# Turned value products on probabilities scaled in place by ScalarE, and the last normalization ahead of the third selection

## Chip, cores and metric

One core of a Trainium2 chip runs the whole kernel, one decoder block for 512 positions. The metric is the device time of one execution in microseconds.

## What is computed

After an input normalization, one projection of the 512 x 1024 stream feeds a diagonal state-space branch and a sparse attention branch; sigmoid gates join them, a second projection and a normalization follow, then a router sends each position to 4 of 32 experts. The parts that the change touches are the attention's softmax and value product, and the router's selection:

```python
logits = einsum('bqhd,bqkhd->bhqk', qb, k_sel) * HEAD_DIM ** -0.5
logits = logits - slopes[None, :, None, None] * dist[:, None]
logits = where((dist >= 0)[:, None], logits, -inf)
p = softmax(logits, axis=-1)
out = einsum('bhqk,bqkhd->bqhd', p, v_sel)          # 8 heads of 64
...
mix = (g_ssm * y_ssm + g_att * y_att) @ w_o
h = layer_norm(alpha * h + mix, ln1_g, ln1_b)
logits = h @ w_router + b_router
top_val, top_idx = top_k(logits, 4)
gates = softmax(top_val, axis=-1)
```

## The kernel before, in words

The program is written out engine by engine; each engine works through its own list in order, and semaphores (`s_...`) order the engines among each other. Positions are tiled by 128 into four query tiles t = 0..3.

Attention (349.6 to 458.1 us) runs over 32 steps i = (t, head). A step's keys are the t + 1 chunks of 128 positions up to its own tile, so its width is 128, 256, 384 or 512 columns. On TensorE: `qk` (L1548) makes the query-key products of two steps at once, each on 64 rows of the array; `probsT` (L1560) transposes the probabilities of a step, chunk by chunk, into bank 7; `pv` (L1570) multiplies the transposed probabilities (stationary, 128 columns) with the values (moving, 64 columns), so the result has queries on partitions; after a query tile's eight heads `o_T` (L1580) transposes its output in four pieces. Between the steps, at every even i, TensorE puts one tile of the gated linear unit (GLU) of the state-space branch: 12 products of 512 columns (L1431 to L1433). On VectorE: `logits` (L1093) adds the distance penalty, takes the row maximum and scales it; after a query tile it takes the reciprocals of the eight sums and multiplies the output with them (L1123, L1126). `value` (L1106) multiplies a GLU tile with its gate. On ScalarE: `exps` (L782) is the exponential with its row sum, `keep_pT` (L790) copies bank 7 to the memory of the transposed probabilities, `take` (L721) is the sigmoid of a GLU gate tile, which needs another activation table than the exponential. The probabilities and their transposes have two buffers each.

The order in the loops is what matters. TensorE at step i: `qk(i)` if i is even, a GLU tile if i is even, `probsT(i - 1)`, `pv(i - 2)`. ScalarE at step i: `exps(i)`, `keep_pT(i - 1)`, and `take` where i % 4 is 3. VectorE at step i: `logits(i)`, and `value` where i % 4 is 1.

The GLU's weights are split by GpSimd into an upper and a lower part (L550, L552), one split for each GLU tile.

After the attention come its output projection (L1437) and the joined output projection `w_out` (L1610), to 541.5 us. VectorE then normalizes tile t (L1171 to L1181), TensorE transposes it and multiplies with the router's weights (`route`, L1626), VectorE selects the four experts (L1188 to L1202), TensorE counts the places (`place`, L1643), and VectorE marks which positions go in the first expert's rows (L1150) and computes the addresses of all (`first_addresses`, L1146, eight small instructions a tile). GpSimd writes a list of positions for each expert by these addresses (`write_first`, L582, four scattered writes a tile, each tile as its addresses come). SyncE loads the finished list, VectorE takes the next block's positions from it (`next_token`, L1280), and only then goes on with the split (`lo`, L1160) of part 7 of the first expert's weights. The first block uses weight parts 4 to 11 (1 MB each): ScalarE rounds the upper part (`hi`, L827), VectorE subtracts it (`lo`), and TensorE multiplies (`up_part`, L1719). `first_rows` (L1659) gathers the first expert's rows by a product with the marks. Then 32 blocks and a last one follow, each with 12 weight parts.

## Time and profile before

| | |
|---|---|
| three runs, median (lowest to highest) | 1761.35 us (1761.05 to 1763.37) |
| the profiled execution, its own time | 1764.82 us |
| its span | 1763.1 us |
| TensorE busy | 1686.9 us, 96% of the span |
| VectorE, ScalarE, GpSimd busy | 1499.1, 1063.4, 467.5 us |
| chain that ended last, by engine | TensorE 87%, VectorE 9%, ScalarE 2% |

The chain is followed back from the last instruction, at each step to what released it. An engine that is not on it may still be idle or busy without changing the end. The granted clock of TensorE is printed as a share of full speed: 1.00 is 2.4 GHz, 0.50 is 1.2 GHz. Instructions overlap a little in the records, so what one costs in a queue is the distance between two starts rather than its own length.

### The profile page before, as it was taken

The page shows a single profiled execution, that of the slowest core. Times are in us where ns is not written, and L with a number is a line of the kernel's source. Part 1 is how long each engine was busy: PE and PEld are TensorE (multiplying, and loading weights), DVE is VectorE, ACT ScalarE, POOL GpSimd, SP SyncE. Part 2 cuts the span into 40 slices and gives each one's busy share as a digit, 9 for nine tenths or more (in the row PEclk, how much of TensorE's full clock was granted, in tenths as well). Part 3 has the DMA queues.
Part 4 walks back from the last instruction along what each step waited for, and adds up shares of the span by engine and source line. Part 5 has one row for each costly group of instructions (what it writes and reads, how often), then busy time and mean ns, then how long its engine had stood idle before and what let it go on. Part 6 is the DMA issues. An engine that isn't in the chain of part 4 may idle for free.

```text
span 1763.1 us, 22201 instructions
## 1 busy us (share of the span) xinstructions
PE 1686.9 (96%) x7129; PEld 1107.8 (63%) x7129; DVE 1499.1 (85%) x1710; ACT 1063.4 (60%) x1016; POOL 467.5 (27%) x298
## 2 busy tenths in 40 slices
PE   5899999999997999999999999999999999999996
PEld 2333344476576577777777777777777777777763
DVE  5999877555568799999999999999999999999995
ACT  4332222365445477777777777777777777777771
POOL 4855000064334111223121212222222212121210
PEclk9999899998998899999999999999999999999998
DMA  5111122110316789999999999999999999999973
GB/s 172 48 51 48 48 76 92 58 48 39 120 45 227 304 308 369 368 366 366 368 382 358 368 365 378 361 365 360 373 365 369 364 371 374 363 355 373 382 293 104
DMA packets 91901, 464.76 MB, mean 264 GB/s; under 512 B 21289, under 2 KB 21405, under 8 KB 42616
## 3 DMA queue, kind: packets, MB, share of 16 engines
q1 hardware_dynamic: 80240, 441.67, 65.9%
q0 software_dynamic: 9776, 18.41, 4.3%
q10 hardware_dynamic: 1848, 4.24, 0.7%
q8 instruction: 17, 0.28, 0.1%
q14 instruction: 20, 0.16, 0.0%
HBM read 454.15 MB, written 18.53 MB: 268 GB/s over the span
## 4 chain that ended last, share of the span: by engine, by line
PE 87%; DVE 9%; ACT 2%; issue 1%; DMA 0%; ACTq 0%; DVEq 0%
PE ps L1715 20%; PE ps L1717 20%; PE ps L1716 20%; PE ps L1515 6%; PE ps L1701 3%; PE ps L1442 2%; PE ps L1437 2%; PE ps L1723 2%; PE ps L1423 2%; PE ps L1431 1%; PE ps L1623 1%; PE ps L1622 1%; PE ps L1621 1%; PE ps L1576 1%; PE ps L1433 1%
## 5 line engine op out<-in xcount | busy, mean ns | idle before, releaser
L1163 DVE TENSOR_TENSOR w_lo<-raw,w_hi 128x2048 fp32r<-128x2048 f32 x384 | 874.1, 2287 | 76.3 <-ACT w_hi L832 76.2
L832 ACT ACTIVATE w_hi<-raw 128x2048 fp32r<-128x2048 f32 x384 | 737.0, 1920 | 244.6 <-PE ps L1717 244.2
L1715 PE MATMUL ps<-w_hi,x_hi 128*96 128x512 f32 x1024 | 415.9, 406 | 0.0
L1717 PE MATMUL ps<-w_lo,x_hi 128*96 128x512 f32 x1024 | 404.7, 395 | 0.0
L1716 PE MATMUL ps<-w_hi,x_lo 128*96 128x512 f32 x1024 | 404.4, 395 | 0.0
L1715 PEld LDWEIGHTS ps<-w_hi,x_hi 128*96 128x96 f32 x1024 | 169.3, 165 | 67.5 <-issue 1.5
L1717 PEld LDWEIGHTS ps<-w_lo,x_hi 128*96 128x96 f32 x1024 | 166.7, 163 | 71.1 <-issue 0.2
L1715 PE MATMUL ps<-w_hi,a_hi 128*96 128x512 f32 x512 | 204.6, 400 | 5.7 <-DVE a_lo L1261 5.7
L1716 PEld LDWEIGHTS ps<-w_hi,x_lo 128*96 128x96 f32 x1024 | 167.0, 163 | 64.0 <-issue 0.2
L1716 PE MATMUL ps<-w_hi,a_lo 128*96 128x512 f32 x512 | 201.8, 394 | 0.0
L604 POOL DMA_INDIRECT gate_now<-gate_rows,row_now x32 | 79.8, 2495 | 458.8 <-DVE tok_out L1291 443.7
L1717 PE MATMUL ps<-w_lo,a_hi 128*96 128x512 f32 x512 | 201.5, 394 | 0.0
L612 POOL DMA_INDIRECT sum_rows<-far,tok_out x31 | 77.2, 2489 | 335.7 <-ACT far L918 335.7
L1442 PE MATMUL ps<-ring 128*128 128x512 f32 x256 | 120.1, 629 | 2.5 <-ACT ring L686 2.0
L1515 PE MATMUL ps<-ring 128*128 128x512 f32 x256 | 111.5, 595 | 0.0
L1715 PEld LDWEIGHTS ps<-w_hi,a_hi 128*96 128x96 f32 x512 | 83.0, 162 | 39.2 <-issue 5.8
L1717 PEld LDWEIGHTS ps<-w_lo,a_hi 128*96 128x96 f32 x512 | 83.1, 162 | 36.3
L1716 PEld LDWEIGHTS ps<-w_hi,a_lo 128*96 128x96 f32 x512 | 83.3, 163 | 33.4
L1442 PEld LDWEIGHTS ps<-ring 128*128 128x128 f32 x256 | 50.8, 202 | 71.6 <-issue 69.3
L596 POOL DMA_INDIRECT scr<-h_rows,tok_now x32 | 70.5, 2205 | 81.3 <-DVE tok_now L1285 74.3
L1515 PEld LDWEIGHTS ps<-ring 128*128 128x128 f32 x256 | 48.2, 190 | 61.5 <-issue 61.2
L918 ACT ACTIVATE far<-ps,gate_now 96x512 f32<-96x512 f32 x64 | 40.3, 678 | 42.7 <-PE ps L1717 42.7
(323 smaller groups left out, 2034.6 us busy)
## 6 DMA issues: line engine op xcount, KB each, us to landing
raw<-in_w_up SPq DMA_DIRECT2D x256, 1024.0 KB, 8.0
raw<-in_w_down SPq DMA_DIRECT2D x128, 1024.0 KB, 9.4
ring<-in_w_in SPq DMA_DIRECT2D x9, 2048.0 KB, 7.8
ring<-in_w_glu SPq DMA_DIRECT2D x4, 1024.0 KB, 6.3
ring<-in_w_o SPq DMA_DIRECT2D x2, 2048.0 KB, 11.7
h<-in_x SPq DMA_DIRECT2D x4, 512.0 KB, 4.9
ring<-in_w_attn_proj SPq DMA_DIRECT2D x1, 2048.0 KB, 8.9
h_rows<-h ACTq DMA_DIRECT2D x4, 512.0 KB, 3.6
```

Source lines behind the costliest of these rows:

```text
L596: g.indirect_dma_start(xg[:, :], None, h1_rows, bass.IndirectOffsetOnAxis(ap=tok_now[:, 0:1], axis=0), bounds_check=last_tok, oob_is_err=F ...
L604: g.indirect_dma_start(gate_now[:, :], None, gate_rows, bass.IndirectOffsetOnAxis(ap=row_now[:, 0:1], axis=0), bounds_check=last_row, oob_ ...
L612: g.indirect_dma_start(sum_rows, bass.IndirectOffsetOnAxis(ap=tok_out[:, 0:1], axis=0), ysb.rearrange("p a b -> p (a b)"), None, bounds_ch ...
L832: s.activation(hi_of(c)[:, :], raw_of(c), ACT.Copy).then_inc(s_hi, 1)
L918: s.activation(ysb[:, r, :], ps[4 + r][0:BLK, :], ACT.Copy, scale=gate_now[:, 0:1]).then_inc(s_ysb, 1)
L1163: d.tensor_tensor(lo_of(c)[:, :], raw_of(c), hi_of(c)[:, :], ALU.subtract).then_inc(s_lo, 1)
L1442: ins = mm(o[:, :], w[:, k, c:c + P], hT[:, k, :], start=k == 0, stop=k == KD - 1)
L1515: ins = mm(ps[n % 2][:, :], gate_weights(g)[:, k, :], hT[:, k, :], start=k == 0, stop=k == KD - 1)
L1701: ins = tr(ps[bank][:, BLK * k:BLK * k + BLK], cols(k), ident[0:BLK, 0:BLK])
L1715: mm(o, xh, hi_of(c)[:, col], start=start, stop=False)
L1716: mm(o, xl, hi_of(c)[:, col], start=False, stop=False)
L1717: return mm(o, xh, lo_of(c)[:, col], start=False, stop=stop)
```

## The change

In the attention the probabilities and their transposes get four buffers each. ScalarE scales each step's probabilities in place by the reciprocal of their sum (`norm`), which VectorE now takes step by step (`inverse`), so that VectorE's normalization of the output and TensorE's transposes of it go. The value products are turned: the values (64 columns) are stationary, the transposed probabilities (128 columns) move, and two heads write to the two halves of the output partitions (`pv_pair`), so that the output comes out transposed. ScalarE copies it once per query tile (`keep_oT`). The orders of the three loops shift: TensorE has the GLU tile at odd i, `probsT(i - 2)` and `pv_pair(i - 4)`; ScalarE has `norm(i - 1)`, `keep_pT(i - 2)` and `take` where i % 4 is 2; VectorE has `inverse(i - 1)` and `value` where i % 4 is 0.

In the routing VectorE normalizes tile 3 right after tile 2, ahead of the selection for tile 2; the marks are parted from the addresses, and the addresses of tiles 1 to 3 are computed together after the last marks, in five wider instructions. ScalarE's and TensorE's lists follow. The dense gates are transposed into bank 4 instead of bank 1, and TensorE waits for them after two weight parts instead of ahead of the first; its wait for the addresses goes.

```diff
@@ -162,8 +162,8 @@
         w_st = [scr[:, 8:12], scr[:, 12:16], ring[:, 5, 1536:3584].rearrange("p (k t) -> p k t", k=4),
                 far[:, :, :], gb[:, :, :].rearrange("p r (k t) -> p (r k) t", k=2)]
         score, relu = scr[:, 0:2], scr[:, 2:4]
-        logit, prob, pT, glu_t = scr[:, 4:6], scr[:, 6:8], scr[:, 8:10], scr[:, 10:12]
-        oq, mix_t = scr[:, 12:13], scr[:, 13:16]
+        logit, glu_t, prob, pT = scr[:, 4:6], scr[:, 6:8], scr[:, 8:12], scr[:, 12:16]
+        mix_t = scr[:, 4:5]
         top8 = sb("top8", [P, 8])
         amax = sb("amax", [P, 2])
         rsum = sb("rsum", [P, TT, HEADS])
...
@@ -782,34 +782,45 @@
             def exps(i):
                 t, hh = STEPS[i]
                 act.wait_ge(s_lg, i + 1)
-                if i >= 2:
-                    act.wait_ge(s_pTp, i - 1)
-                s.activation(prob[:, i % 2, 0:NQT[t]], logit[:, i % 2, 0:NQT[t]], ACT.Exp, scale=HD ** -0.5,
+                if i >= 4:
+                    act.wait_ge(s_pTp, i - 3)
+                s.activation(prob[:, i % 4, 0:NQT[t]], logit[:, i % 2, 0:NQT[t]], ACT.Exp, scale=HD ** -0.5,
                              bias=amax[:, i % 2:i % 2 + 1], accum_out=rsum[:, t, hh:hh + 1]).then_inc(s_pr, 1)
 
             def keep_pT(i):
                 t, hh = STEPS[i]
                 act.wait_ge(s_pTp, i + 1)
-                if i >= 2:
-                    act.wait_ge(s_pv, i - 1)
-                s.activation(pT[:, i % 2, 0:NQT[t]], ps[7][:, 0:NQT[t]], ACT.Copy).then_inc(s_pT, 1)
+                if i >= 4:
+                    act.wait_ge(s_pv, (i - 4) // 2 + 1)
+                s.activation(pT[:, i % 4, 0:NQT[t]], ps[7][:, 0:NQT[t]], ACT.Copy).then_inc(s_pT, 1)
+
+            def norm(i):
+                t, hh = STEPS[i]
+                act.wait_ge(s_inv, i + 1)
+                s.activation(prob[:, i % 4, 0:NQT[t]], prob[:, i % 4, 0:NQT[t]], ACT.Copy,
+                             scale=rinv[:, hh:hh + 1]).then_inc(s_pn, 1)
+
+            def keep_oT(t):
+                act.wait_ge(s_pv, HEADS // 2 * (t + 1))
+                s.activation(qiT[:, :, P * t:P * t + P], ps[2 + t % 2][:, :].rearrange("p (k q) -> p k q", k=4),
+                             ACT.Copy).then_inc(s_oT, 1)
 
             for i in range(len(STEPS) + 2):
                 if i < len(STEPS):
                     exps(i)
                 if 1 <= i <= len(STEPS):
-                    keep_pT(i - 1)
-                if i % 4 == 3 and n < first_tile["at"]:
+                    norm(i - 1)
+                if i >= 2:
+                    keep_pT(i - 2)
+                if i % 4 == 2 and n < first_tile["at"]:
                     take(n)
                     n += 2
-                if i >= 2 and STEPS[i - 2][1] == HEADS - 1:
-                    t = STEPS[i - 2][0]
-                    act.wait_ge(s_oTp, t + 1)
-                    s.activation(qiT[:, :, P * t:P * t + P], ps[3][:, :].rearrange("p (k q) -> p k q", k=4),
-                                 ACT.Copy).then_inc(s_oT, 1)
+                if i >= 11 and STEPS[i - 11] == STEPS[HEADS * ((i - 11) // HEADS)]:
+                    keep_oT((i - 11) // HEADS)
             while n < first_tile["at"]:
                 take(n)
                 n += 2
+            keep_oT(TT - 1)
...
-            for t in range(TT):
+            def std(t):
                 act.wait_ge(s_var, TT + t + 1)
                 s.activation(rsx[:, t, 0:1], mvx[:, t, 1:2], ACT.Sqrt, bias=eps[:, 0:1]).then_inc(s_rstd, 1)
-                if t == 1:
-                    act.wait_ge(s_bs, 1)
-                    step(s.activation(bias3[third, :], braw_b[third, :], ACT.Copy))
-                    s.activation(brem[third, :], bias3[third, :], ACT.Copy).then_inc(s_bc, 1)
-                if t == 2:
-                    step(s.activation(bias3[second, :], braw_b[second, :], ACT.Copy))
-                    act.wait_ge(s_bs, 2)
-                    s.activation(bias3[third, :], braw_b[third, :], ACT.Copy).then_inc(s_b3l, 1)
-                if t == 3:
-                    for c in range(4, 6):
-                        hi(-1, c)
+
+            def rows_off(t):
                 act.wait_ge(s_h1, t + 1)
                 act.dma_start(h1_rows.rearrange("(t p) d -> p t d", p=P)[:, t, :], h[:, t, :]).then_inc(s_h1row, 16)
+
+            def keep_hT1(t):
                 for r in range(2):
                     act.wait_ge(s_h1T, 2 * t + r + 1)
                     if t > 0:
                         act.wait_ge(s_lgt, t)
                     s.activation(hT1[:, 4 * r:4 * r + 4, :], ps[6 + r][:, :].rearrange("p (k q) -> p k q", k=4),
                                  ACT.Copy).then_inc(s_h1e, 1)
+
+            def gate_exps(t):
                 act.wait_ge(s_v8, t + 1)
                 s.activation(all_exp[:, t, :], lg[:, :], ACT.Exp, bias=gneg[:, 0:1])
                 s.activation(gates[:, t, :], rt8[:, t, 0:TOPK], ACT.Exp, bias=gneg[:, 0:1],
                              accum_out=gsum[:, 0:1]).then_inc(s_ge, 1)
+
+            std(0)
+            rows_off(0)
+            keep_hT1(0)
+            gate_exps(0)
+            std(1)
+            act.wait_ge(s_bs, 1)
+            step(s.activation(bias3[third, :], braw_b[third, :], ACT.Copy))
+            s.activation(brem[third, :], bias3[third, :], ACT.Copy).then_inc(s_bc, 1)
+            rows_off(1)
+            keep_hT1(1)
+            gate_exps(1)
+            std(2)
+            step(s.activation(bias3[second, :], braw_b[second, :], ACT.Copy))
+            act.wait_ge(s_bs, 2)
+            s.activation(bias3[third, :], braw_b[third, :], ACT.Copy).then_inc(s_b3l, 1)
+            rows_off(2)
+            keep_hT1(2)
+            std(3)
+            gate_exps(2)
+            rows_off(3)
+            keep_hT1(3)
+            hi(-1, 4)
+            gate_exps(3)
+            hi(-1, 5)
+
...
@@ -1103,6 +1135,11 @@
                 d.tensor_scalar(amax[:, i % 2:i % 2 + 1], top8[:, 0:1], -HD ** -0.5, None, ALU.mult).then_inc(s_lg, 1)
                 dve.wait_ge(s_lg, i + 1)
 
+            def inverse(i):
+                t, hh = STEPS[i]
+                dve.wait_ge(s_pr, i + 1)
+                d.reciprocal(rinv[:, hh:hh + 1], rsum[:, t, hh:hh + 1]).then_inc(s_inv, 1)
+
             def value(i):
                 n = first_tile["gg"] + 2 * i + 1
                 dve.wait_ge(s_tile, n + 1)
@@ -1114,19 +1151,10 @@
             for i in range(len(STEPS) + 2):
                 if i < len(STEPS):
                     logits(i)
-                if i % 4 == 1 and i > 1:
+                if 1 <= i <= len(STEPS):
+                    inverse(i - 1)
+                if i % 4 == 0 and i > 0:
                     value(i // 4 - 1)
-                if i >= 2 and STEPS[i - 2][1] == HEADS - 1:
-                    t = STEPS[i - 2][0]
-                    dve.wait_ge(s_pv, i - 1)
-                    dve.wait_ge(s_pr, i - 1)
-                    step(d.reciprocal(rinv[:, :], rsum[:, t, :]))
-                    if t > 0:
-                        dve.wait_ge(s_oTp, t)
-                    d.tensor_tensor(oq.rearrange("p o (h e) -> p (o h) e", h=HEADS),
-                                    ps[2][:, :].rearrange("p (h e) -> p h e", h=HEADS),
-                                    rinv[:, :].unsqueeze(2).to_broadcast([P, HEADS, HD]), ALU.mult).then_inc(s_on, 1)
-                    dve.wait_ge(s_on, t + 1)
...
-            def first_addresses(t):
+            def first_marks(t):
 
                 dve.wait_ge(s_pos, t + 1)
                 step(d.tensor_copy(pos[:, t, :], ps[1][:, 0:NE]))
                 d.tensor_scalar(in_first[:, t, :], tcol[:, 0:BLK], pos[:, t, 0:1], chosen[:, t, 0:1], ALU.is_equal,
                                 ALU.mult).then_inc(s_inf, 1)
-                ad, picked = adw[:, t, 0, :], adw[:, t, 1, :]
-                step(d.scalar_tensor_tensor(ad, pos[:, t, :], float(NE), tcol[:, 0:NE], ALU.mult, ALU.add))
...
-                d.tensor_copy(addr_i[:, TOPK * t:TOPK * t + TOPK], addr[:, t, :]).then_inc(s_adr, 1)
-                dve.wait_ge(s_adr, t + 1)
+
+            def first_addresses(t0, t1):
+
+                shape = [P, t1 - t0, TOPK, NE]
+                ad = adw[:, t0:t1, 0, :]
+                picked = part_lo[:, 0:(t1 - t0) * TOPK * NE].rearrange("p (t k e) -> p t k e", k=TOPK, e=NE)
+                step(d.scalar_tensor_tensor(ad, pos[:, t0:t1, :], float(NE),
+                                            tcol[:, 0:NE].unsqueeze(1).to_broadcast([P, t1 - t0, NE]), ALU.mult, ALU.add))
+                step(d.tensor_tensor(picked, tcol[:, 0:NE].unsqueeze(1).unsqueeze(1).to_broadcast(shape),
+                                     rif[:, t0:t1, 0:TOPK].unsqueeze(3).to_broadcast(shape), ALU.is_equal))
+                step(d.tensor_tensor(picked, picked, ad.unsqueeze(2).to_broadcast(shape), ALU.mult))
+                step(d.reduce_sum(addr[:, t0:t1, :], picked, AXL.X))
+                d.tensor_copy(addr_i[:, TOPK * t0:TOPK * t1], addr[:, t0:t1, :].rearrange("p t k -> p (t k)"))\
+                    .then_inc(s_adr, t1 - t0)
+                dve.wait_ge(s_adr, t1)
...
@@ -1180,10 +1216,8 @@
                 step(d.scalar_tensor_tensor(h[:, t, :], h[:, t, :], mvx[:, t, 0:1], gb[:, 0, :], ALU.subtract, ALU.mult))
                 d.scalar_tensor_tensor(h[:, t, :], h[:, t, :], rsx[:, t, 1:2], gb[:, 1, :], ALU.mult, ALU.add)\
                     .then_inc(s_h1, 1)
-                if t > 0:
-                    first_addresses(t - 1)
-                if t == TT - 1:
-                    lo(-1, 4)
+
+            def choose(t):
                 dve.wait_ge(s_lgt, t + 1)
                 d.tensor_tensor(lg[:, :], b_rt[:, :], ps[0][:, 0:NE], ALU.add).then_inc(s_lgfree, 1)
                 dve.wait_ge(s_lgfree, t + 1)
@@ -1202,7 +1236,22 @@
                 d.scalar_tensor_tensor(all_exp[:, t, :], all_exp[:, t, :], gsum[:, 1:2], chosen[:, t, :], ALU.mult,
                                        ALU.mult).then_inc(s_gd, 1)
                 dve.wait_ge(s_gd, t + 1)
-            first_addresses(TT - 1)
+
+            norm1(0)
+            choose(0)
+            norm1(1)
+            first_marks(0)
+            first_addresses(0, 1)
+            choose(1)
+            norm1(2)
+            norm1(3)
+            first_marks(1)
+            choose(2)
+            first_marks(2)
+            choose(3)
+            first_marks(3)
+            first_addresses(1, TT)
+            lo(-1, 4)
 
             cnt, more, upto_e, t0 = rw[:, 0, :], rw[:, 1, :], rw[:, 2, :], rw[:, 3, :]
...
@@ -1559,31 +1608,26 @@
 
             def probsT(i):
                 t, hh = STEPS[i]
-                pe.wait_ge(s_pr, i + 1)
+                pe.wait_ge(s_pn, i + 1)
                 if i >= 1:
                     pe.wait_ge(s_pT, i)
                 for c in range(t + 1):
-                    ins = tr(ps[7][:, P * c:P * c + P], prob[:, i % 2, P * c:P * c + P], ident[:, :])
+                    ins = tr(ps[7][:, P * c:P * c + P], prob[:, i % 4, P * c:P * c + P], ident[:, :])
                 ins.then_inc(s_pTp, 1)
                 return ins
 
-            def pv(i):
+            def pv_pair(i):
                 t, hh = STEPS[i]
-                pe.wait_ge(s_pT, i + 1)
-                if hh == 0 and t > 0:
-                    pe.wait_ge(s_on, t)
+                pe.wait_ge(s_pT, i + 2)
+                if hh == 0 and t > 1:
+                    pe.wait_ge(s_oT, t - 1)
                 for c in range(t + 1):
-                    ins = mm(ps[2][:, HD * hh:HD * hh + HD], pT[:, i % 2, P * c:P * c + P],
-                             v[:, c, HD * hh:HD * hh + HD], start=c == 0, stop=c == t)
+                    for j in (i, i + 1):
+                        rows = slice(HD * (j % 2), HD * (j % 2) + HD)
+                        ins = mm(ps[2 + t % 2][rows, P * (hh // 2):P * (hh // 2) + P],
+                                 v[:, c, HD * (hh + j - i):HD * (hh + j - i) + HD],
+                                 pT[:, j % 4, P * c:P * c + P], start=c == 0, stop=c == t)
                 ins.then_inc(s_pv, 1)
-
-            def o_T(t):
-                pe.wait_ge(s_on, t + 1)
-                if t > 0:
-                    pe.wait_ge(s_oT, t)
-                for k in range(4):
-                    ins = tr(ps[3][:, P * k:P * k + P], scr[:, 12, P * k:P * k + P], ident[:, :])
-                ins.then_inc(s_oTp, 1)
 
             pe.wait_ge(s_gelu, 4)
             pe.wait_ge(s_far, TT - 1)
@@ -1591,15 +1635,13 @@
             for i in range(len(STEPS) + 3):
                 if i < len(STEPS) and i % 2 == 0:
                     qk(i)
-                if i % 2 == 0 and i > 0 and n < first_tile["at"]:
+                if i % 2 == 1 and n < first_tile["at"]:
                     tile(n, 9 + (n - first_tile["gg"]) // 8)
                     n += 1
-                if 1 <= i <= len(STEPS):
-                    probsT(i - 1)
-                if 2 <= i <= len(STEPS) + 1:
-                    pv(i - 2)
-                if i >= 3 and STEPS[i - 3][1] == HEADS - 1:
-                    o_T(STEPS[i - 3][0])
+                if 2 <= i < len(STEPS) + 2:
...
@@ -1655,7 +1699,8 @@
                 if t > 1:
                     place(t - 2)
                 if t > 0:
-                    route(t - 1)
+                    route_T(t - 1)
+                    route_lg(t - 1)
             def first_rows(t):
 
...
@@ -1668,13 +1713,14 @@
                     if t == TT - 1:
                         ins.then_inc(s_tr, 1)
 
-            place(TT - 2)
             pe.wait_ge(s_wofree, 6)
             for half in range(2):
                 mm(ps[2 + half][:, 0:4 * BLK], ones_b[:, :], none_b[:, :], start=True, stop=False)
             first_rows(0)
+            route_T(TT - 1)
+            place(TT - 2)
+            route_lg(TT - 1)
             first_rows(1)
-            route(TT - 1)
             first_rows(2)
             place(TT - 1)
             first_rows(3)
@@ -1684,7 +1730,7 @@
...
@@ -1757,11 +1803,10 @@
             pe.wait_ge(s_tlo, 2)
             pe.wait_ge(s_b3, 1)
             pe.wait_ge(s_b3l, 1)
-            pe.wait_ge(s_adr, TT)
-            pe.wait_ge(s_gdTe, 1)
             for p in range(8):
                 up_part(-1, p + 4, p)
                 if p == 1:
+                    pe.wait_ge(s_gdTe, 1)
                     pe.wait_ge(s_bias, 64)
                     gated_biases(0)
                     gated_biases(1)

```

## Rows read from the trace of the kernel before

**Rows 1.** Busy us of each engine in stretches, then clock, DMA share, GB/s.

```profile
349.60:458.10 108.50, 97.22 (x514) 74.98 (x513) 53.72 (x120) 60.60 (x125) 51.24 (x40) 0.92 0.14 50
350.10:352.30 2.20, 0.04 (x3) 0.01 (x1) 1.45 (x6) 2.17 (x5) 2.05 (x3) 1.00 0.58 141
378.80:382.20 3.40, 3.40 (x9) 2.62 (x9) 1.92 (x6) 3.00 (x5) 0.00 (x0) 0.53 0.01 2
402.70:409.50 6.80, 6.80 (x22) 4.84 (x21) 2.52 (x6) 4.53 (x8) 6.57 (x4) 0.51 0.00 0
433.40:440.30 6.90, 6.90 (x19) 4.41 (x19) 3.05 (x6) 4.42 (x6) 0.00 (x0) 0.51 0.00 0
650.00:1000.00 350.00, 350.00 (x1614) 248.99 (x1613) 332.46 (x334) 260.59 (x197) 80.95 (x37) 1.00 0.98 368
```

**Rows 2.** TensorE in order of time: start, length, operation, [idle before, releaser].

```profile
352.29 0.33 PE L1566 MATMUL ps<-ident,scr 128*128 128x128 f32 x1 [2.17 <-ACT scr L787]
...
377.19 0.41 PE L1566 MATMUL ps<-ident,scr 128*128 128x128 f32 x2 [1.54 <-ACT scr L795]
...
402.42 0.52 PE L1566 MATMUL ps<-ident,scr 128*128 128x128 f32 x3 [1.75 <-ACT scr L795]
...
432.58 0.63 PE L1566 MATMUL ps<-ident,scr 128*128 128x128 f32 x4 [1.96 <-ACT scr L795]
```

**Rows 3.** Chain that ended last, 429 to 460: start, length, engine, line.

```profile
443.90 1.06 PE ps L1556 x4
...
447.93 0.44 PE ps L1566 x4
448.36 0.84 PE ps L1576 x8
```

**Rows 4.** TensorE in order of time, state-space products at 200 us.

```profile
200.04 0.59 PE L1488 MATMUL ps<-far,ring 128*32 128x512 f32 x1
...
200.47 0.59 PE L1488 MATMUL ps<-far,ring 128*32 128x512 f32 x1
```

**Rows 5.** ScalarE in order of time, three stretches.

```profile
67.38 0.71 ACT L695 ACTIVATE v<-tcol,spw 128x512 f32<-128x512 f32 x1
68.00 0.71 ACT L696 ACTIVATE ring<-tcol,spw 128x512 f32<-128x512 f32 x1
...
357.23 1.28 ACT L730 ACT_TABLE_LOAD   x1
...
360.44 0.40 ACT L787 ACTIVATE scr<-scr,amax 128x128 f32<-128x128 f32 x1
...
431.15 0.71 ACT L787 ACTIVATE scr<-scr,amax 128x512 f32<-128x512 f32 x1
...
431.85 0.58 ACT L795 ACTIVATE scr<-ps 128x512 f32<-128x512 f32 x1
432.33 0.72 ACT L787 ACTIVATE scr<-scr,amax 128x512 f32<-128x512 f32 x1
...
446.69 0.72 ACT L787 ACTIVATE scr<-scr,amax 128x512 f32<-128x512 f32 x1 [3.00 <-DVE amax L1103]
```

**Rows 6.** GpSimd in order of time, first split and list writes.

```profile
350.56 1.26 POOL L552 TENSOR_TENSOR wg_lo<-ring,wglu_hi 128x512 fp32r<-128x512 f32 x1
...
567.27 5.24 POOL L586 DMA_INDIRECT first_list<-code,addr_i  x1 [0.31 <-issue]
572.81 0.98 POOL L586 DMA_INDIRECT first_list<-code,addr_i  x1 [0.30 <-issue]
```

**Rows 7.** VectorE in order of time, routing and first block.

```profile
553.49 1.29 DVE L1181 SCALAR_TENSOR_TENSOR h<-h,rsx,gb 128x1024 f32<-128x1024 f32 x1
...
578.95 0.15 DVE L1284 COPY slot_now<-slots 96x1 int32<-96x1 int32 x1 [2.83 <-DMA slots<-first_list]
```

**Rows 8.** TensorE in order of time, first expert block.

```profile
569.12 1.03 PE L1723 MATMUL ps<-bias,pick 96*96 96x512 bf16 x4 [2.49 <-ACT scr L881]
...
586.48 0.63 PE L1715 MATMUL ps<-w_hi,x_hi 128*96 128x512 f32 x1
```

19 lines of the change are left out of this document (10 added, 9 removed).

## Prediction

> **What bounds the kernel now.** I read the busy times of one long stretch first, then the chain that ended last, then single engines in order of time. From 650 us on TensorE is busy all the time at full clock (350.00 of 350 us in the first such stretch [rows 1]), and nothing in the diff touches that part: the expert blocks simply start earlier or later. So the sum is made of two stretches. In the attention (349.6 to 458.1) TensorE is busy 97.2 of 108.5 us, ScalarE 60.6, VectorE 53.7 [rows 1]; the chain is nearly all TensorE there. Its few stalls matter twice. Stalls of 1.54, 1.75 and 1.96 us [rows 2] are each followed by a stretch at a granted clock of about half (0.53, 0.51, 0.51, that is 1.2 instead of 2.4 GHz) [rows 1], while one of 2.17 us at 350 us [rows 2] was not: that stretch shows 1.00. The lost time is (1 - clock) x length: 0, 1.6, 3.3 and 3.4 us, 2.1 on average. The second stretch is the routing, from the end of the output projection (541.5) to the first expert product at 569.1, and the part of the first block that still waits for it (to about 587).
>
> **Attention: what is removed and added on TensorE.** A value product of one head and one 128-key chunk is two instructions (160 for the 80 products of L1576), eight of them in 0.84 us [rows 3], 0.105 us each, 16.8 us in all; a 64-column stream would be shorter than that, so the weight load of 128 columns sets it. Turned, the load has 64 columns and the stream 128, and the two heads of a pair write different halves of the output partitions. Four 32-column products of the state-space part start within 0.01 us of each other, the next four 0.43 us later [rows 4]: column groups run side by side. A quarter of that stream is 0.107 us. Lower bound for a pair's pass: 0.107 us, 80 passes, 8.6 us; upper: 0.21 (no overlap), 16.8 us, no gain. I take 0.125 us, 10 us: near the lower end, as the side-by-side row is the same kind of product. The 16 transposes of the output go as well (four per query tile, as long as those of a step, 0.44 us [rows 3], 1.8 us), with the wait for VectorE's normalization and ScalarE's copy behind which the three stalls above stood. So TensorE sheds about 9 us of work.
>
> The Trainium skill, "TensorEngine Tiling (Array Packing)", Key Properties, has independent tiles that load and multiply in parallel, but says that changing the tiling mode drains the engine. By that rule the turned products would take their lower bound and something more at each of the 16 pairs for the drain, which neither the page nor a row here prices; on the parallel tiles the trace agrees [rows 4].
>
> **Attention: what is added on ScalarE.** 32 scaled copies in place. A copy scaled by a per-partition number over 512 columns is followed 0.61 us later by the next [rows 5]; by width that is about 0.29, 0.40, 0.50 and 0.61 us for the four query tiles, 14.4 us in all. Busy time would still be only 60.6 + 14.4 = 75 of 108 us, which looks free. It is not, for the order of the queue. A sigmoid for a GLU tile costs two table loads: from the first load to the next exponential 3.21 us (357.23 to 360.44) [rows 5]. Before, it stands after an odd step, and the next exponential waits for the next query-key products anyway. After, it stands after step i = 2, 6, 10, ...: on ScalarE come exp(i), norm(i-1), copy(i-2), the sigmoid, exp(i+1), norm(i), copy(i-1), and the transpose of step i needs norm(i) and copy(i-1). TensorE reaches that transpose one GLU tile and one pair of query-key products after the products of step i.
>
> For query tile 3, from the end of the products of step i: 1.73 us to its exponential (443.90 + 1.06 to 446.69) [rows 3, 5]; exponential 0.70, scaled copy 0.61, copy 0.48 (431.15, 431.85, 432.33) [rows 5]; sigmoid 3.21; exponential 0.70, scaled copy 0.61, full copy 0.60, semaphore 0.05: 8.7 us. Beside it TensorE has a transpose 0.44, products 1.0, GLU tile 2.95, transpose 0.44, query-key 1.06 [rows 3]: 5.9 us. It stalls 2.8 us, then does another 5.9: four steps take 14.6 us, where the work alone is 11.8. For tile 0, by its narrower instructions (exponential 0.40 [rows 5]), the same sum is 1.0 + 0.40 + 0.29 + 0.17 + 3.21 + 0.40 + 0.29 + 0.28 + 0.05 = 6.1 against 3.8 us of work: stall 2.3, period 9.9. Tiles 1 and 2 lie between: 11.5 and 13.0.
>
> VectorE's 32 one-column reciprocals (0.15 us each, 5 us) stand between the logits of two steps; it is idle over half the stretch, and they only matter inside the chain above, where logits(i+1) covers them.
>
> The sum: the first GLU tile now comes before the second pair of products and waits for GpSimd's first split, done at 351.8 [rows 6]; the products of step 2 end at 355.1. Seven periods from step 2 to 30: 9.9 + 10.6 + 11.5 + 12.2 + 13.0 + 13.8 + 14.6 = 85.6, to 440.7. Then 8.7 of chain and 3.8 of tail (two transposes, two copies, the last products 0.9, the copy of the output): 453.2, against 458.1. At full clock the change wins 4.9 us. But it has seven stalls of 2.3 to 2.8 us before its tail, each longer than the three that halved the clock. At 2.1 us each they cost 14.7. (The clock after the tail's stall falls in both.) Attention: -4.9 + 14.7 = +9.8 us; bounds -4.9 (the clock stays) and +19 (each costs 3.4).
>
> **Routing.** The last normalization now follows the third directly: its end moves from 554.8 [rows 7] to about 547.2, since VectorE can start when the last projection is done (541.4). Selection 3, 3.4 us, and selection 4 follow, each with its share of TensorE and ScalarE waits; the last gather into the first block begins near 559 instead of 562.6, and with selection 4 out of the way of the split x_lo is ready near 564. The table load for the square root between them goes too. The wait for the dense gates moves behind two weight parts. So the first expert product starts at about 564.5 instead of 569.1 [rows 8]: -4.6 us.
>
> What is given back: addresses of tiles 1 to 3 are now computed together, after the last marks, about 560.5. The saving on VectorE (three times about 1.6 us against 2.3) is small, but the 12 scattered list writes of GpSimd wait for them all. Before, five of these twelve were issued by then. A write takes 0.98 us [rows 6], with 0.3 between two, and the one that met VectorE's two long splits took 5.24 us and ended 0.9 after them. Twelve writes from 561.3, blocked by the split of part 4 (to 563.8) and by those of parts 5 and 6 (to 569.3), end near 582 instead of 573.8. VectorE's token step, released by the list's load, came 5.2 us after the last write's end (573.79 to 578.95) [rows 6, 7]; VectorE waits there ahead of the split of part 7. That split moves from 581.5 to about 590. TensorE, which began part 7's product at 586.48 without waiting [rows 8], would now be ready at 581.5 and wait until 590: +3.6 us, with the clock falling once more, of which VectorE's own pace (2.3 us a part and 1.3 for each sum) hides most: +4 at the end of the block. Lower bound, if the writes aren't blocked: 0.7 us earlier than before; upper, with the slow clock on the path: +6.
>
> **Sum.** +9.8 + 4 = +14 us. The profiled execution took 1764.8 (span 1763.1) and would take 1778.6; it lies 3.5 above the median of 1761.35, so I predict 1775.
>
> **Rivals.**
> Stalls without their price (0.14): ScalarE's chain stalls TensorE, but the clock stays at 2.4 GHz, as after the 2.17 us at 350. -4.9 + 4: 1760 (1756 to 1763).
> The other side (0.14): TensorE's work decides. If the sigmoid with its two loads doesn't come between exp(i) and exp(i+1) on the path (for instance since ScalarE runs ahead of TensorE by more than I find), the 3.21 us are hidden. Periods are then 7.6 to 11.8 us, stretch end 9 after 351.9 + 77.6, or 438.5: -19.6; with +4, 1746, and 1740 to 1750 with the bounds of the routing. It decides as soon as the stall is under some 1 us. For it speaks ScalarE's busy share, 75 of 108; against it its fixed order.
> Every stall costs 3.4 us and the routing 6 (0.12): +25, 1786, up to 1792.
> The Trainium skill, "ScalarE: Activation LUTs", What ACT_TABLE_LOAD costs, gives 1.28 us for a load and 1.38 for a drain at each change of set. By it the sigmoid would hold the queue 5.97 us, and the eight places would add some 20 us more, 1795. The trace doesn't agree: two loads and a sigmoid of 0.60 fill 3.21 us [rows 5] with no gap for a drain, so its chance is under 0.01.
>
> **Numbers.** Main case 0.60: 1775, own range 1765 to 1786. The range 1755 to 1788 takes in the second case and most of the heavy one, and leaves out the TensorE case. A measurement tells 0.2% (3.5 us) from no change. Slower: 0.60 + 0.12 = 0.72; same: 0.07 (half of the second case); faster: 0.21 (the TensorE case and the rest of the second).
>
> **What would show it.** Right: TensorE idle 2 to 3 us ahead of the transposes of steps 2, 6, ..., 30, released by ScalarE's copy, with ScalarE's two table loads just before; granted clock under 0.85 over the attention; eight pairs of table loads as before; list writes all after 560 and VectorE waiting some 10 us for the list. Wrong: sixteen half-periods near 3.8 to 5.9 us, or a granted clock near 1.00 in spite of stalls; pairs of turned products at 0.21 us a pass; the token step before 582.

## The result, and the profile after

The changed kernel takes 1778.09 us (median of 5 executions, 1772.93 to 1781.04) against 1761.05 (5 executions, 1758.70 to 1763.37) for the kernel before: a ratio of 1.0091, 95% interval 1.0073 to 1.0109. It is slower by 17 us; 1775 was predicted, with a range of 1755 to 1788. Its profiled execution took 1777.87 us (span 1776.1, 13.0 more than the span before). The 4 us between 17 and 13 are not in the two traces: the profiled execution of the kernel before lies 3.8 us above its median of 1761.05, that of the changed kernel lies at its median.

The 13.0 us of the two traces divide as follows. The attention starts at 350.79 instead of 349.63 (+1.2; work in front of it that the diff doesn't touch). It lasts 116.5 us instead of 108.45 (+8.1). From its end to the last product of the output projection it is 82.2 instead of 83.1 us (-0.9). From there to the start of expert block 0 it is 72.6 instead of 68.1 (+4.5). From 650 us on the stretch looks as before [rows 1]: TensorE 350.00 of 350 us busy.

Busy time of the engines in stretches of the kernel after (columns as in [rows 1]: PE, PEld, DVE, ACT, POOL, granted clock, DMA share, GB/s):

```profile
350.80:467.30 116.50, 92.58 (x498) 64.71 (x497) 54.94 (x144) 75.20 (x158) 50.20 (x40) 0.89 0.20 70
363.20:366.70 3.50, 3.50 (x12) 2.61 (x13) 1.42 (x5) 1.05 (x5) 3.26 (x4) 0.59 0.00 0
...
414.00:418.00 4.00, 4.00 (x21) 3.02 (x22) 3.78 (x5) 1.93 (x6) 3.92 (x2) 0.59 0.00 0
...
374.60:378.60 4.00, 4.00 (x22) 2.82 (x22) 2.80 (x6) 1.87 (x8) 1.44 (x2) 1.00 0.01 2
...
458.50:470.00 11.50, 8.72 (x43) 5.76 (x44) 1.46 (x3) 4.81 (x10) 1.60 (x2) 0.50 1.05 385
```

TensorE's own work fell from 97.2 to 92.6 us, ScalarE's rose from 60.6 to 75.2, and the stretch got longer. The gap is in the group of the transposes, and in single places (kernel after, TensorE: the group in the attention, then four rows in order of time):

```profile
L1615 PE MATMUL ps<-ident,scr 128*128 128x128 f32 x80 | 16.1, 303 | 20.7 <-ACT scr L795 20.6
```

```profile
374.50 0.30 PE L1615 MATMUL ps<-ident,scr 128*128 128x128 f32 x1 [1.70 <-ACT scr L795]
...
443.36 0.63 PE L1615 MATMUL ps<-ident,scr 128*128 128x128 f32 x4 [2.99 <-ACT scr L795]
443.92 1.41 PE L1627 MATMUL ps<-scr,v 128*64 128x128 f32 x16
...
459.90 1.09 PE L1615 MATMUL ps<-ident,scr 128*128 128x128 f32 x4 [3.83 <-ACT scr L795]
```

Before, the same group waited 9.5 us in all [rows 2]. Now it waits 20.6 us, in eight places: 2.57, 1.70, 2.47, 2.05, 2.74, 2.30, 2.99 and 3.83 us, at every fourth step. Behind five of them the clock falls (the stretches at 363.2, 387, 400, 414 and 445, granted 0.59 to 0.63 on average; 0.50 is its lower level); behind 1.70 and 2.30 it doesn't; behind the last it is 0.50 to the end of the attention. What ScalarE does ahead of the stall that ends at 443.36 (in order of time):

```profile
436.18 0.72 ACT L787 ACTIVATE scr<-scr,amax 128x512 f32<-128x512 f32 x1 [2.21 <-DVE amax L1135]
...
436.90 0.71 ACT L800 ACTIVATE scr<-scr,rinv 128x512 f32<-128x512 f32 x1
437.52 0.57 ACT L795 ACTIVATE scr<-ps 128x512 f32<-128x512 f32 x1
438.11 1.28 ACT L730 ACT_TABLE_LOAD   x1
439.40 0.60 ACT L730 ACTIVATE scr<-ps 128x512 f32<-128x512 f32 x1
440.02 1.28 ACT L787 ACT_TABLE_LOAD   x1
441.31 0.72 ACT L787 ACTIVATE scr<-scr,amax 128x512 f32<-128x512 f32 x1
...
442.03 0.71 ACT L800 ACTIVATE scr<-scr,rinv 128x512 f32<-128x512 f32 x1
442.65 0.57 ACT L795 ACTIVATE scr<-ps 128x512 f32<-128x512 f32 x1
```

That is the chain of the prediction, item by item: exponential, scaled copy, copy, load, sigmoid, load, exponential, scaled copy, copy, without a gap for 7.0 us. TensorE waits for its last row.

The routing of the kernel after, three engines, each in order of time (GpSimd's list writes, VectorE, TensorE):

```profile
571.52 2.41 POOL L586 DMA_INDIRECT first_list<-code,addr_i  x1 [26.69 <-DVE addr_i L1192]
574.24 5.37 POOL L586 DMA_INDIRECT first_list<-code,addr_i  x1 [0.31 <-issue]
...
591.47 0.98 POOL L586 DMA_INDIRECT first_list<-code,addr_i  x1 [0.30 <-issue]
```

```profile
554.66 1.28 DVE L1217 SCALAR_TENSOR_TENSOR h<-h,rsx,gb 128x1024 f32<-128x1024 f32 x1
...
567.98 0.19 DVE L1177 COPY pos<-ps 128x32 f32<-128x32 f32 x1 [4.08 <-PE ps L1693]
...
595.40 0.15 DVE L1333 COPY slot_now<-slots 96x1 int32<-96x1 int32 x1 [11.94 <-DMA slots<-first_list]
```

```profile
574.40 1.94 PE L1769 MATMUL ps<-bias,pick 96*96 96x512 bf16 x4 [3.25 <-DVE x_lo L1310]
...
597.99 0.74 PE L1761 MATMUL ps<-w_hi,x_hi 128*96 128x512 f32 x1 [8.86 <-DVE w_lo L1199]
...
622.14 1.94 PE L1769 MATMUL ps<-bias,pick 96*96 96x512 bf16 x4 [3.77 <-DVE x_lo L1310]
```

These answer to [rows 6 to 8]. VectorE waits 11.94 us for the list (before 2.83), and TensorE 8.86 us for the weight split that stands on VectorE behind it (before not at all).

### The profile page after: what moved, and what is told of

Same layout as the page of the kernel before. It is cut to its first block, busy times and chain, and to the rows that moved or that the text cites. A ratio compares the mean times of both kernels' runs of the same rounds, so it can differ in the third digit from the quotient of the medians.

```text
span 1776.1 us, 22209 instructions
## 1 busy us (share of the span) xinstructions
PE 1680.5 (95%) x7113; PEld 1096.4 (62%) x7113; DVE 1498.5 (84%) x1704; ACT 1075.6 (61%) x1047; POOL 468.3 (26%) x298
## 4 chain that ended last, share of the span: by engine, by line
PE 84%; DVE 9%; ACT 3%; issue 2%; POOL 1%; DMA 1%; ACTq 0%; DVEq 0%; POOLq 0%
PE ps L1761 20%; PE ps L1763 20%; PE ps L1762 20%; PE ps L1564 6%; PE ps L1747 3%; PE ps L1491 2%; PE ps L1486 2%; PE ps L1769 2%; PE ps L1472 2%; PE ps L1663 1%; PE ps L1665 1%; PE ps L1664 1%; DVE scr L1069 1%; DVE scr L1070 1%; PE ps L1480 1%
## 5 line engine op out<-in xcount | busy, mean ns | idle before, releaser
L1761 PEld LDWEIGHTS ps<-w_hi,a_hi 128*96 128x96 f32 x512 | 83.1, 162 | 39.4 <-issue 5.8
L1491 PEld LDWEIGHTS ps<-ring 128*128 128x128 f32 x256 | 50.3, 200 | 70.8 <-issue 68.6
L950 ACT ACTIVATE far<-ps,gate_now 96x512 f32<-96x512 f32 x64 | 40.3, 679 | 43.7 <-PE ps L1763 43.7
```

Source lines behind the costliest of these rows:

```text
L950: s.activation(ysb[:, r, :], ps[4 + r][0:BLK, :], ACT.Copy, scale=gate_now[:, 0:1]).then_inc(s_ysb, 1)
L1491: ins = mm(o[:, :], w[:, k, c:c + P], hT[:, k, :], start=k == 0, stop=k == KD - 1)
L1761: mm(o, xh, hi_of(c)[:, col], start=start, stop=False)
```

## The experiments

The theory has two halves. ScalarE's chain, with the sigmoid and its two table loads between two exponentials, stalls TensorE, and the stalls cost clock as well; and in the routing, all twelve list writes wait for one late address step. The rivals: the turned products are slow in themselves, the clock falls for another reason, or the loss lies in only one of the two parts. This table is worked out from the traces. Attention: from its first query-key product to the attention projection. Stalls: idle time of TensorE ahead of the step transposes (line 1615 and its like), released by ScalarE. The last three columns are us from the start of the last output product to the first expert product, to the start of the last list write, and to the first product of block 0.

| kernel | median us | ratio to before (95%) | attention | stalls | expert | last write | block 0 |
|---|---|---|---|---|---|---|---|
| before | 1761.05 | | 108.5 | 9.5 | 27.9 | 31.6 | 68.1 |
| after | 1778.09 | 1.0091 (1.0073-1.0109) | 116.5 | 20.6 | 24.9 | 41.9 | 72.6 |
| e1_sigmoid_odd | 1756.85 | 0.9976 (0.9959-0.9993) | 99.6 | 7.8 | 24.9 | 42.0 | 72.7 |
| e2_addresses_early | 1771.31 | 1.0062 (1.0039-1.0084) | 116.6 | 20.7 | 24.0 | 33.4 | 64.3 |
| e3_both | 1747.53 | 0.9934 (0.9910-0.9959) | 99.0 | 7.8 | 24.2 | 32.2 | 64.4 |
| e4_filled_stall | 1768.70 | 1.0044 (1.0030-1.0058) | 109.1 | 6.7 | 24.9 | 42.0 | 72.6 |
| e7_routing_only | 1762.49 | 1.0006 (0.9989-1.0023) | 108.8 | 9.5 | 23.3 | 40.3 | 71.9 |
| e8_attention_only | 1769.75 | 1.0049 (1.0029-1.0070) | 116.5 | 20.7 | 28.6 | 27.4 | 68.6 |
| e9_token_later | 1776.96 | 1.0066 (1.0042-1.0090) | 119.4 | 20.6 | 24.9 | 45.6 | 72.4 |
| e10_all_three | 1747.16 | 0.9902 (0.9878-0.9925) | 101.1 | 8.4 | 26.9 | 33.6 | 65.5 |
| e5_no_scaling | 1866.58 | 1.0584 (1.0555-1.0613) | 102.2 | 13.4 | 23.3 | 40.3 | 71.9 |
| e6_no_table_loads | 1752.78 | 0.9948 (0.9932-0.9964) | 95.0 | 7.7 | 23.3 | 40.3 | 71.9 |
| e11_routing_early | 1758.26 | 0.9980 (0.9966-0.9994) | 105.5 | 9.5 | 26.6 | 33.4 | 66.6 |
| e12_attention_odd | 1754.37 | 0.9942 (0.9920-0.9964) | 99.9 | 7.8 | 28.7 | 27.6 | 68.5 |

Each ratio is to executions of the kernel before taken beside it on the same chip (medians 1761.09, 1762.59 and 1761.80). The changed kernel was not run again beside them. So "us less than the changed kernel" below compares medians taken on different chips, and the ratios give somewhat other sizes: 20 us for the sigmoid's place, 5 for the addresses, 28 for both, 8 for the filled stalls, 4 for the token step. The attention of the kernel with the token step moved is longer (119.4 us) because it is at the lower clock for more of the time: 0.86 against 0.89 on average.

**The sigmoid's place.** On the changed kernel:

```diff
-                if i % 4 == 2 and n < first_tile["at"]:
+                if i % 4 == 3 and n < first_tile["at"]:
```

> The changed kernel, with the sigmoid of a GLU tile and its two table loads moved from behind even steps (2, 6, 10, ...) to behind odd ones (3, 7, 11, ...), as in the kernel before. Theory (ScalarE's fixed order stalls TensorE, and the stalls cost clock): the sigmoid now stands behind an odd step, after which ScalarE next waits for query-key products anyway, so the chain exponential, scaled copy, copy, sigmoid, exponential, scaled copy, copy no longer stands ahead of one transpose. The eight stalls of 1.70 to 3.83 us (20.6 us in the changed kernel) fall under about 0.5 us each, the five stretches at half clock go, and the attention, 116.5 us long in the changed kernel, takes 96 to 102 us: 14 to 20 us less, 1758 to 1764 us in all. Rival A (the stall moves with the sigmoid, since its 3.2 us must be paid somewhere between two pairs): stalls of 1.5 to 3 us stay, at the odd steps' transposes, and the time stays within 5 us of 1778. Rival B (the stalls go, but the turned products are slow in themselves): 6 to 10 us less only, with a granted clock of 1.00 in the attention.

Measured: 1756.85 us, 21 less than the changed kernel and just under the expected 1758; in the traces 16.9 less of attention and 15.7 less of span. The stalls at the transposes fall from 20.6 to 7.8 us, though not all below 0.5 as expected: the longest left are 1.44 and 1.35, and 3.9 us in front of GLU tiles are new. Only the last is followed by a slow stretch. One condition in the order of a queue carries the whole loss and more, so rivals A and B fall.

**Filling the stall.** On the changed kernel, ahead of the transpose, eight products whose result nobody reads:

```diff
+                if i % 4 == 0 and 4 <= i < len(STEPS):
+                    pe.wait_ge(s_lg, i)
+                    for _ in range(8):
+                        mm(ps[QK_BANKS[(i + 2) % 3]][:, :], u_hi[:, 1, 0:P], u_hi[:, 0, :], start=True, stop=True)
```

> The changed kernel, with eight products of 512 columns, whose results nothing reads, issued by TensorE ahead of the transpose at which it stalls, in seven of the eight places (steps 4, 8, ..., 28 of the query-key order and what lies between). They add work, no result changes. They fill about 1.9 us of each stall of 1.7 to 3 us. Theory (what a stall costs is its own length, and after it a stretch at half clock of some 1.7 us): the order of ScalarE is unchanged, so the transposes come at the same time or at most 0.3 us later, but the clock no longer falls after them; the five stretches near 0.6 go, and the attention takes 5 to 8 us less than 116.5: 1770 to 1773 us. Rival A (the clock falls for another reason than the idle time, the turned products or the load itself): the granted clock of the attention stays near 0.89 and the time goes up by 0 to 6 us. Rival B (the clock's fall lies beside ScalarE's chain, which sets the period alone): the clock goes back to 1.00 and the time stays within 2 us of 1778.

Measured: 1768.70, 9.4 us less, slightly below the expected 1770. Two groups of TensorE in the attention, and the busy times of 100 us of it:

```profile
L1615 PE MATMUL ps<-ident,scr 128*128 128x128 f32 x80 | 15.5, 295 | 6.7 <-ACT scr L795 6.7
L1644 PE MATMUL ps<-u_hi 128*128 128x512 f32 x56 | 14.8, 406 | 0.0
```

```profile
351.00:451.00 100.00, 92.69 (x508) 64.45 (x508) 52.18 (x142) 71.27 (x152) 50.09 (x39) 1.00 0.14 49
```

56 products without a use make the kernel faster. They are busy for 14.8 us, and TensorE's stalls at the transposes shrink from 20.6 to 6.7 us. ScalarE's order is unchanged, and the granted clock over these 100 us is 1.00 where the changed kernel has 0.91. That is the price of the falls alone: 7.4 us of attention. Rival A, a fall for another reason than the idle time, is refused by the clock. Rival B, by which ScalarE's chain sets the period whatever the clock, would have given nothing. It overlooks that the chain starts at the end of TensorE's products, which the low clock puts off; that reading is argued from the order of the queues and was not tried by itself. The unfilled last stall, 3.82 us, keeps its slow tail.

**Without the scaled copies** (this leaves out the softmax division; the mixture is then another one, and more work follows, presumably since other experts are chosen: from 1000 us to 1850 us TensorE runs 3855 matmuls, against 3327 in the next kernel, which has ended by then. Only the attention can be compared, not the total):

```diff
-                s.activation(prob[:, i % 4, 0:NQT[t]], prob[:, i % 4, 0:NQT[t]], ACT.Copy,
-                             scale=rinv[:, hh:hh + 1]).then_inc(s_pn, 1)
+                act.sem_inc(s_pn, 1)
```

> The changed kernel without the 32 scaled copies in place; this leaves out the softmax division, everything else keeps its place and order. Theory (the two scaled copies between a step's products and the transpose at which TensorE stalls are part of the chain): each of the eight stalls gets shorter by two copies, 0.6 us for tile 0 up to 1.2 us for tile 3: 2.99 us becomes 1.8, 2.57 becomes 2.0, the sum of 20.6 us becomes 13 to 14. The attention of 116.5 us takes 109 to 110, or less where the clock doesn't fall after the shorter stalls: 1763 to 1771 us. Rival (the chain begins at VectorE's logits and the copies lie beside it): the stalls keep their length within 0.3 us, and the time stays within 3 us of 1778.

The total of 1866.58 misses the expectation for the reason above, which I had not thought of. The stalls are as expected: TensorE's row that answers to 2.99 us is

```profile
432.28 0.63 PE L1614 MATMUL ps<-ident,scr 128*128 128x128 f32 x4 [1.76 <-ACT scr L795]
```

and the sum is 13.4 us. Two copies per stall, 1.23 us here. The attention takes 102.2 us, 14.3 less: 7.2 from the stalls themselves, and about as much from fewer slow stretches (clock 0.96 over the attention).

**Without the table loads** (a plain copy in place of the sigmoid; the sigmoid of these tiles is left out):

```diff
-                    ins = s.activation(glu_t[:, i % 2, :], src[:, :], ACT.Sigmoid)
+                    ins = s.activation(glu_t[:, i % 2, :], src[:, :], ACT.Copy)
```

> The changed kernel with a plain copy in place of the sigmoid of the first GLU half; this leaves out the sigmoid of these eight tiles, and with it sixteen table loads of 1.28 us. The order on ScalarE stays. Theory (the two loads are what makes the chain longer than the work beside it): every chain is 2.6 us shorter, the eight stalls, 20.6 us in all, shrink to 0 to 0.5 us each, the clock stays at full speed, and the attention takes 96 to 100 us instead of 116.5: 1755 to 1762 us. Rival A (the loads hide beside the wait for the logits): at least half of each stall stays, 1768 or more. Rival B (each change of table holds the queue for longer than the load itself, as a drain of 1.38 us, which the Trainium skill states in ScalarE: Activation LUTs, What ACT_TABLE_LOAD costs): the chain is 5 us shorter, which shows only in the last stall, the one of 3.83 us, since the others are used up before: it goes to 0.

Measured: 1752.78, attention 95.0 us, a little less than expected, and rival A (1768 or more) falls. What two loads hold is read from ScalarE's queue around the last sigmoid, from one exponential to the next. First the changed kernel, then this one:

```profile
452.71 0.73 ACT L787 ACTIVATE scr<-scr,amax 128x512 f32<-128x512 f32 x1 [2.10 <-DVE amax L1135]
...
457.85 0.72 ACT L787 ACTIVATE scr<-scr,amax 128x512 f32<-128x512 f32 x1
```

```profile
435.19 0.72 ACT L787 ACTIVATE scr<-scr,amax 128x512 f32<-128x512 f32 x1 [0.68 <-DVE amax L1135]
...
437.48 0.72 ACT L787 ACTIVATE scr<-scr,amax 128x512 f32<-128x512 f32 x1
```

5.14 - 2.29 = 2.85 us, for two loads of 1.28. Rival B, with a drain at each change, wanted about 5. The Trainium skill has a drain of 1.38 us per change of set beside its 1.28 us for the load ("ScalarE: Activation LUTs", What ACT_TABLE_LOAD costs). The load is there in this queue, the drain isn't. The last stall, by which rival B was to be tested, could not have told: it fell from 3.83 to 0.78 us (TensorE, then ScalarE of the kernel without loads), and there ScalarE's copy waits for the transposes of the step before, so that a still shorter chain would have left the same stall.

```profile
440.51 0.63 PE L1615 MATMUL ps<-ident,scr 128*128 128x128 f32 x4 [0.78 <-ACT scr L795]
```

```profile
439.77 0.60 ACT L795 ACTIVATE scr<-ps 128x512 f32<-128x512 f32 x1 [0.87 <-PE ps L1615]
```

But 7.7 us of stalls stay, up to 2.08 us, where 0 to 0.5 at each of eight places were expected. In one of them ScalarE waits for VectorE, which is busy with the gate of the GLU tile between two steps' logits (VectorE of this kernel, in order of time):

```profile
390.61 0.69 DVE L1147 TENSOR_TENSOR scr<-scr,ps 128x512 f32<-128x512 f32 x1
391.34 1.85 DVE L1149 TENSOR_TENSOR ring<-ring,scr 128x512 f32<-128x512 f32 x1
393.22 0.55 DVE L1132 SCALAR_TENSOR_TENSOR scr<-far,ps 128x384 f32<-128x384 f32 x1
```

So with the table loads gone that stall, the longest, is set by VectorE; this is read from these rows, and no kernel took the gate's product away.

**Each part alone.** The kernel before with only the hunks of one part.

> The kernel before with the attention's part of the change alone: turned value products, scaled copies in place, the sigmoid behind even steps; the routing is that of the kernel before. Theory: 8 us more than before for the attention (116.5 instead of 108.5 us), 0 to 1 us more or less behind it: 1769 to 1770 us, ratio 1.0047. Rival A (the routing swallows part of a later attention, since GpSimd's first split and the weights don't wait for it): 1763 to 1766. Rival B (all of the loss is here): 1774 to 1778.

> The kernel before with the part of the change that lies in the routing alone: last normalization ahead of the third selection, marks and addresses taken apart, dense gates later; the attention is that of the kernel before. Theory (from the changed kernel's trace: block 0 starts 12.9 us late, 8.5 of it already there at the end of the output projection): 4.4 us more than before, 1765.5 us, ratio 1.0025. The first expert product comes 3 us earlier and part 7's product 3 us later than before. Rival A (the routing gains what it was meant to, and the 4.4 us are a consequence of the later attention): 1758 to 1761. Rival B (all of the loss is here): 1775 or more.

Measured: the attention alone 1.0049 (+8.6 us), as expected; the routing alone 1.0006, +1.1 us, interval -1.9 to +4.1. The expected 4.4 lies just outside, the +3.8 of its trace (71.9 against 68.1 to block 0) just inside; its single executions run from 1759.41 to 1771.71. The two parts add to +9.7 by their medians, while both together give +16 by the ratio; the intervals allow it, and the traces do (8.1 + 3.8). So the attention is the larger part and surely a loss; the routing is 4 us by every trace and cannot be told from zero by the times. Rival A of the routing, a loss that only follows from the later attention, is refused by its trace alone, which has the 3.8 us behind the attention of the kernel before. Its first expert product does come earlier, and its list later (TensorE of the routing-only kernel):

```profile
565.49 1.06 PE L1769 MATMUL ps<-bias,pick 96*96 96x512 bf16 x4 [3.25 <-DVE x_lo L1303]
...
589.09 0.74 PE L1761 MATMUL ps<-w_hi,x_hi 128*96 128x512 f32 x1 [10.42 <-DVE w_lo L1192]
```

**Addresses earlier.**

```diff
+            first_addresses(1, 3)
             choose(3)
             first_marks(3)
-            first_addresses(1, TT)
+            first_addresses(3, TT)
```

> The changed kernel, with the addresses of query tiles 1 and 2 computed right behind the marks of tile 2, ahead of the selection of tile 3, and only those of tile 3 behind the last marks; attention as in the changed kernel. Theory (the list writes are late because all twelve wait for one address computation, and the first block's part 7 waits for the list): eight of the twelve writes go out from about 561, the last one ends near 585 instead of 592.5, VectorE's token step moves from 595.4 to about 588, part 7's first product waits 2 to 3 us instead of 8.86, and block 0 starts about 7 us earlier: 1771 us, 0.4% less than the changed kernel. Rival A (GpSimd's writes are blocked by VectorE's splits wherever they stand): the eight early writes take about 5 us each, the last write still ends past 590, and the time stays within 2 us of 1778. Rival B (the extra address step delays selection 4 and the first expert product by its own 1.6 us, and no more is won at part 7 than is lost there): within 2 us as well, but with the last write near 585.

> The kernel before with the routing's part of the change and the addresses of tiles 1 and 2 ahead of selection 4; attention as before. Theory (moving the last normalization ahead of the third selection wins some 3 us at the first expert product, and only the joint addresses give it away at part 7): block 0 starts 5 to 7 us earlier than with the routing part alone, and 2 to 4 us earlier than before: 1757 to 1760 us, ratio 0.9975 to 0.999. Rival (the reordering itself wins nothing at the start of block 0, which VectorE's splits and the weights set): 1761 to 1763, though part 7 doesn't wait.

Measured: on the changed kernel 6.8 us less (1771.31), on the routing alone 4.2 less (1758.26, ratio 0.9980). The last write comes 33.4 us after the output projection instead of 41.9, no product of part 7 waits, and block 0 starts 8.4 us earlier. GpSimd of the first of these kernels, the seventh to ninth of its twelve writes:

```profile
568.94 3.07 POOL L586 DMA_INDIRECT first_list<-code,addr_i  x1 [0.30 <-DVE addr_i L1192]
572.32 5.37 POOL L586 DMA_INDIRECT first_list<-code,addr_i  x1 [0.30 <-issue]
577.99 0.98 POOL L586 DMA_INDIRECT first_list<-code,addr_i  x1 [0.31 <-issue]
```

Two writes are still held, 3.07 and 5.37 us, where they meet the long splits; what is won is that six are done before them, 1.28 us from one to the next. Rival A falls, and rival B too, since the first expert product isn't later (24.0 against 24.9). In the kernel with the routing alone the first expert product comes only 26.6 us after; there TensorE's gather has a gap of 2.14 us for which the trace names no releaser. That stays open.

**The token step later.**

```diff
-            dve.wait_ge(s_slots, 16)
-            next_token(1)
...
+                if c == 8:
+                    dve.wait_ge(s_slots, 16)
+                    next_token(1)
```

> The changed kernel, with VectorE's wait for the list of slots and its first token step moved from ahead of part 7's weight split to behind it. The writes themselves are as in the changed kernel. Theory (part 7's product waits for a split that stands on VectorE behind the list): part 7's first product no longer waits 8.86 us but under 3, and block 0 starts 5 to 8 us earlier: 1770 to 1773. Rival A (block 0's gather of its rows needs the token step just as early, so that the wait moves to block 0's first product): the time stays within 2 us of 1778. Rival B (the free VectorE blocks GpSimd's writes for longer, the last one ends past 595): part of the gain only, 1774 to 1777.

Measured: 1776.96 (1.0066), no gain beyond the interval, and in the trace 0.2 us at block 0. What rival A and rival B describe is both there (TensorE, then GpSimd):

```profile
600.56 0.74 PE L1762 MATMUL ps<-w_hi,x_hi 128*96 128x512 f32 x1 [5.07 <-DVE w_lo L1199]
...
620.86 1.94 PE L1770 MATMUL ps<-bias,pick 96*96 96x512 bf16 x4 [5.75 <-DVE x_lo L1310]
```

```profile
583.97 2.52 POOL L586 DMA_INDIRECT first_list<-code,addr_i  x1 [0.30 <-issue]
586.79 3.10 POOL L586 DMA_INDIRECT first_list<-code,addr_i  x1 [0.30 <-issue]
```

The wait moves one part on (8.86 becomes 5.07) and to block 0 (3.77 becomes 5.75), and the freed VectorE, now splitting while the list is written, holds two more writes: the last comes 3.7 us later. My theory took the place of the wait for its cause.

**The versions put together.**

> The kernel before with the attention's part of the change and the sigmoid behind odd steps, where it was; routing as before. Theory (the turned products win about 9 us of attention once ScalarE's chain is off the path): the attention takes 99 to 101 us instead of 108.5, and the end of block 0 follows: 1750 to 1754 us, ratio 0.9945. Rival (the routing as before can't use an earlier attention, since something else, weights or GpSimd, sets block 0's start): 1758 or more.

> Both edits on the changed kernel: the sigmoid behind odd steps, and the addresses of tiles 1 and 2 ahead of selection 4. The two lie in different stretches (attention, and routing with the first expert block), so theory: the savings add, 20 to 27 us less than the changed kernel, 1751 to 1758, which is 0.2 to 0.6% under the kernel before (1761). Rival (the sigmoid's place gives nothing): 1771. Rival (neither gives anything): 1778.

> Three edits on the changed kernel: the sigmoid behind odd steps, the addresses of tiles 1 and 2 ahead of selection 4, and the token step behind part 7's split. Theory: attention 14 to 20 us less, routing and first block 8 us less (the second and the third edit work on the same wait of 8.86 us, so they don't add fully): 1750 to 1756. Rival (the second and third edits add, since one removes the late writes and the other the wait): 1744 to 1750. Rival (the third edit only moves the wait to block 0): equal to the kernel with two edits within 1.5 us.

Measured: 1754.37, 1747.53 and 1747.16 us. The first is just above what was expected; the second lies below its range, 31 us under the changed kernel where 21 and 7 would add to 28. In its trace the output projection behind the attention, which stays at full clock, takes 78.4 us instead of 82.2, and that is what goes beyond the two edits. All three are faster than the kernel before, by 0.6, 0.7 and 1.0%. The third edit adds nothing that the traces show (block 0 at 65.5 against 64.4); its ratio is the lowest, but the intervals of the last two overlap. The best version is thus the whole change with the first two edits.

The kernel with the odd sigmoid alone and the one with both edits have the same attention code and the same stall of 1.35 us before its end. They show how loosely stall and clock hang together. Busy times from 450 to 455, first with the odd sigmoid alone, then with both edits:

```profile
450.00:455.00 5.00, 4.31 (x11) 1.85 (x8) 0.00 (x0) 1.75 (x3) 1.56 (x2) 0.50 1.06 392
```

```profile
450.00:455.00 5.00, 5.00 (x13) 2.19 (x12) 1.38 (x2) 1.63 (x4) 2.53 (x2) 1.00 1.05 397
```

## Why the prediction was right, and where it was not

**The mechanism held.** Eight stalls at the named transposes, released by the named copy, with the two loads just before; moving the sigmoid took most of them away (20.6 to 7.8 us). The chain was put at 8.7 us for query tile 3 and took 8.9, from the end of the query-key products at 434.50 to the transpose at 443.36; the two copies in it had the forecast size.

**TensorE's work, mis-sized a little.** A pass of a pair (one instruction for each of its two heads; 128 keys take two passes) was put at 0.125 us. At full clock, all data ready, 16 instructions take the 1.03 us between the two rows below (TensorE, both edits), 0.129 us a pass; in the changed kernel itself the same 16 were stretched to 1.4 us by the low clock.

```profile
429.85 1.09 PE L1628 MATMUL ps<-scr,v 128*64 128x128 f32 x16
430.88 0.50 PE L1481 MATMUL ps<-u_hi,wglu_hi 128*128 128x512 f32 x1
```

The lower bound of [rows 4], two column groups fully side by side, was 0.107; the pair lies 0.17 us in all above it. Ahead of the pair the transposes take 0.59 us from start to start (429.26 to 429.85), where before the same four transposes ahead of products of the whole array took 0.47 (442.42 to 442.89). The Trainium skill has a drain at a change of tiling mode, without a price ("TensorEngine Tiling (Array Packing)", Key Properties). The trace allows one of at most about 0.3 us at this pair of query tile 3, behind and ahead of it together.

**The full-clock length of the attention, 2.5 us too low.** Predicted 103.6 (349.63 to 453.2). Measured 116.5, less 7.7 us for five slow stretches ((1 - clock) x length: 1.4, 1.5, 1.7, 1.6, 1.5) and 2.7 for the slow tail (its first transposes and products 2.9 us instead of 1.6, its last ones 4.5 instead of 3.1, the shorter numbers from the kernel with both edits): 106.1. The stalls were put at 2.3 to 2.8 us and came at 1.70 to 2.99, alternating; the last, put at 2.8, took 3.83: I had set query-key products of a next pair beside it (1.06 us), and the last pair has none behind it. The tail behind it, put at 3.8, took 4.7 without the slow clock. These two are 1.9 of the 2.5 us.

**The clock, 4.3 us too high.** Predicted seven falls at 2.1 us; there were five at 1.5 us, and the tail, which I had set equal in both, cost 2.7 more: 10.4 instead of 14.7. The errors of 2.5 and -4.3 us cancel in part: +8.1 instead of +9.8 us. That is luck, and so is some of the nearness of 1775 to 1778.

**Routing.** Normalization 4 ended 6.4 us after the output projection's last product (predicted 6.0). The first expert product was won by 3.1 us instead of 4.6: I had both selections follow at once, but VectorE waits 4.08 us for the places of tile 3, which stand on TensorE behind two tiles' gather of 32 products. In the routing-only kernel it was 4.7. The last write ended 42.9 us after the projection (I had 40.8): two writes were held, 2.41 and 5.37 us, ten went at 1.28. The token step came 2.95 us after it, not 5.2. Part 7's product: +3.2 (predicted +3.6). Start of block 0: +4.5 (+4).

**From trace to median.** The sum was made for the profiled execution, 1778.6 against 1777.87 measured. I took 3.5 us off for the median; the changed kernel's median is 1778.09. Single executions of one kernel differ by several us, and part of that can be seen: the kernel before has 108.5 us of attention in one trace and 105.5 in the routing kernel with the same attention. The mean granted clock goes with it: of the six executions of the kernel with both edits, the four with 0.982 or 0.983 took 1746.7 to 1747.7 us, the two with 0.977 took 1752.4 and 1754.1.

**The rivals.** "TensorE's work decides" fell, but its price was wrong too: with the sigmoid out of the way I had the attention at 88.9 us, and it took 99.0 to 99.9, and 95.0 even without loads. I had not looked for the next limits, VectorE's gate of the GLU tile and ScalarE's exponential waiting for the logits. At full clock the turned products are worth little: 99.0 against 108.5 - 8.3 = 100.2 us before, since the idle time of TensorE rose from 11.3 to 15.4 us as its work fell. Nearly all of the 9 us by which the repaired attention beats the one before is clock that it no longer loses. "Stalls without their price" is what filling the stalls comes near to, and it was refused by 7.4 us.

## What to carry to other kernels

An engine's busy share says nothing on whether work can be added to it: ScalarE had over 40% of the attention free before (60.6 of 108.5 us busy), and what decided was a sigmoid with two table loads between two exponentials that another engine waits for. Write out the queue from the end of one product to the transpose that needs it, with every table load, and compare it with the work beside it; if it is longer, look first at which half-step the expensive item stands in. When small steps are joined to save instructions, ask who was already being served by the first of them, and move the source of a late result rather than the wait for it.

## What the runs showed of the hardware

Stalls of TensorE bring falls of its clock (with the seven stalls filled, the five falls were gone), but the length of a stall doesn't settle whether one follows. The same stall of 1.75 us, in the same attention code, was followed by 0.50 in the kernel before and by 1.00 in the routing kernel with early addresses:

```profile
403.00:407.00 4.00, 4.00 (x13) 2.56 (x13) 1.17 (x3) 3.63 (x4) 3.84 (x3) 0.50 0.00 0
```

```profile
401.00:405.00 4.00, 4.00 (x21) 2.90 (x20) 2.35 (x5) 3.94 (x5) 3.84 (x3) 1.00 0.00 0
```

Likewise a stall of 1.70 us was followed by 1.00 (changed kernel, 374.6) and one of 1.72 us by 0.60 (the kernel with the token step moved, 372 to 376). So a sum that charges each stall is an average, and a single trace can be 3 us off in it. What decides between the two was not tried.

GpSimd's list writes of 0.98 us (1.28 from one to the next) take longer beside VectorE's splits of 128x2048 elements (2.28 us each). In the fourteen kernels here thirty writes took 1.9 us or more: 1.91 to 3.10 with one split beside them, 4.50 to 5.37 with two on end. Every one of them ended 0.85 or 0.86 us after the end of the split. So fixed a distance in thirty cases speaks for a wait until the split is done; no kernel took the splits away, and what the two engines share there was not tried.
